# Hyena token convolution: a second fold on 128 rows for the even frequencies, and the filter folds moved ahead of the spectral products

## The reference

```python
def two_sided_fft_conv(u, h_fwd, h_bwd, bias):
    L = u.shape[1]
    kern = jnp.concatenate([h_fwd, jnp.zeros((1, h_fwd.shape[1]), F32), h_bwd[:0:-1]], axis=0)
    uf = u.astype(F32)
    spec = jnp.fft.rfft(uf, n=2 * L, axis=1) * jnp.fft.rfft(kern, n=2 * L, axis=0)[None]
    y = jnp.fft.irfft(spec, n=2 * L, axis=1)[:, :L]
    return (y + uf * bias.astype(F32)).astype(u.dtype)

def hyena_mixer(h, w_in, b_in, short_w, short_b, w1, b1, w2, b2, w3, freq, filt_bias, w_out, b_out):
    L = h.shape[1]
    u = centred_depthwise_conv(h @ w_in + b_in, short_w, short_b)
    v, x1, x2 = jnp.split(u, 3, axis=-1)
    filt = hyena_filters(L, w1, b1, w2, b2, w3, freq)
    z = x1 * two_sided_fft_conv(v, filt[:, 0, 0], filt[:, 0, 1], filt_bias[0])
    z = x2 * two_sided_fft_conv(z, filt[:, 1, 0], filt[:, 1, 1], filt_bias[1])
    return z @ w_out + b_out
```

## Time and profile before

| | us |
|---|---|
| median of 3 runs | 3149.48 (3149.09 to 3150.06) |
| the profiled execution | 3147.32 |
| its span in the trace | 3144.8 |
| PE busy over the span | 2980.0 (95%) |
| DVE busy over the span | 1515.3 (48%) |
| ACT busy over the span | 734.2 (23%) |

### The profile page before, as it was taken

The page is one execution under the profiler, slowest core; times in us unless marked ns, Lnnn a source line. Parts: engine busy times, 40 slices in busy tenths (PEclk is TensorE's granted clock), DMA queues, the critical chain, the costliest instruction groups (busy, mean ns, idle before and its releaser), DMA issues.

```text
span 3144.8 us, 36839 instructions
## 1 busy us (share of the span) xinstructions
PE 2980.0 (95%) x14719; PEld 1696.5 (54%) x14719; DVE 1515.3 (48%) x2905; ACT 734.2 (23%) x1539; POOL 419.9 (13%) x262
## 2 busy tenths in 40 slices
PE   8999899999889899899998999999999987999998
PEld 5888443787744377447756433333345544444443
DVE  5994852898393357775565211211144752111212
ACT  1211541121163221112124111000025642111111
POOL 3554000655200142000001100000000000000000
PEclk9999999999999899999999999999999999999999
DMA  5452002447200322011412899999922004999997
GB/s 227 152 210 81 28 1 108 150 183 279 81 1 14 135 84 110 34 54 37 159 67 86 330 398 399 374 390 378 394 116 78 4 3 174 417 421 421 421 421 291
DMA packets 89899, 606.12 MB, mean 193 GB/s; under 512 B 10808, under 2 KB 11611, under 8 KB 19204
## 3 DMA queue, kind: packets, MB, share of 16 engines
q1 hardware_dynamic: 79776, 575.70, 45.8%
q0 software_dynamic: 4432, 15.73, 1.7%
q10 hardware_dynamic: 5524, 12.35, 1.1%
HBM read 592.73 MB, written 11.01 MB: 192 GB/s over the span
## 4 chain that ended last, share of the span: by engine, by line
PE 63%; DVE 7%; ACT 2%; issue 1%; ACTq 0%; DMA 0%; DVEq 0%; PEldq 0%
PE ps L3054 7%; PE ps L3016 7%; PE ps L1451 4%; PE ps L3067 4%; PE ps L3033 4%; PE ps L3097 4%; PE ps L1098 3%; PE ps L1600 3%; PE ps L3361 2%; PE ps L2904 2%; PE ps L1701 2%; PE ps L3106 2%; PE ps L2820 2%; PE ps L2921 2%; PE ps L1972 2%; PE ps L3525 1%
## 5 line engine op out<-in xcount | busy, mean ns | idle before, releaser
L617 PE MATMUL ps<-mem 128*128 128x256 f32 x1792 | 393.1, 381 | 12.9 <-DVE mem L647 10.8
L617 PEld LDWEIGHTS ps<-mem 128*128 128x128 f32 x1792 | 340.1, 191 | 65.3 <-DVE mem L647 14.4
L562 POOL TENSOR_TENSOR mem<-mem 128x512 f32<-128x512 f32 (+1 forms) x160 | 299.5, 1872 | 535.9 <-DVE mem L858 274.6
L760 DVE SCALAR_TENSOR_TENSOR mem<-mem 128x1024 f32<-128x1024 f32 x160 | 256.5, 1644 | 14.4 <-DMA mem<-in_ada_w 13.9
L3054 PE MATMUL ps<-mem 128*64 128x512 f32 x1024 | 223.3, 594 | 0.0
L3016 PE MATMUL ps<-mem 128*64 128x512 f32 x1024 | 222.5, 592 | 0.7 <-ACT mem L2950 0.7
L647 DVE TENSOR_TENSOR mem<-ps,mem 128x256 f32<-128x256 f32 x308 | 121.5, 419 | 111.7 <-PE ps L617 68.2
L1098 PE MATMUL ps<-mem 128*128 128x512 f32 x384 | 169.6, 597 | 1.8 <-DVEq L156 1.8
L3218 DVE TENSOR_TENSOR mem<-ps,mem 128x512 f32<-128x512 f32 x16 | 11.1, 692 | 313.7 <-PE ps L3016 313.7
L3054 PEld LDWEIGHTS ps<-mem 128*64 128x64 f32 x1024 | 72.1, 137 | 150.5 <-issue 150.5
L3016 PEld LDWEIGHTS ps<-mem 128*64 128x64 f32 x1024 | 74.4, 137 | 145.6 <-issue 144.7
(11 more groups left out here) (455 smaller groups left out, 4393.9 us busy)
## 6 DMA issues: line engine op xcount, KB each, us to landing
mem<-in_moe_w SPq DMA_DIRECT2D x384, 1024.0 KB, 15.3
mem<-in_w_in SPq DMA_DIRECT2D x48, 1024.0 KB, 7.2
mem<-in_ada_w SPq DMA_DIRECT2D x48, 1024.0 KB, 5.0
mem<-in_hy_w_in SPq DMA_DIRECT2D x24, 1024.0 KB, 7.0
mem<-in_w_out SPq DMA_DIRECT2D x12, 1024.0 KB, 6.0
mem<-in_k_win_l SPq DMA_DIRECT2D x8, 1024.0 KB, 6.9
mem<-in_hy_w_out SPq DMA_DIRECT2D x8, 1024.0 KB, 4.9
mem<-in_sw_w_in SPq DMA_DIRECT2D x6, 1024.0 KB, 8.2
```

The costliest lines, as they stand in the source:

```text
L562: gp(out, x, y, op).then_inc(A.mark(sem), 1)
L617: m = mm(seven(l, unit), x[:, k, :], y[:, k, :], start=(k == 0), stop=(k == 3))
L760: stt(PRODUCT if again else w, w, 1.0, C_ROWS[:, z, :], ALU.mult, ALU.mult, accum_out=mod(layer, b // KD, b % KD, z))\
```

## The change

For the even frequencies the 256 folded rows are symmetric about their middle a second time, up to a sign that depends on which half of the even frequencies is meant. So the kernel now orders the even frequencies by their parity (first every other one, then the rest), stores the second tile of 128 rows mirrored (`place`, in the tables and the window; `pe_filter` reads the taps of tile 1 from the mirrored array, and `fold` writes the second 128 places of the data reversed), and forms the sum and the difference of the two tiles. An even output then needs one matmul over 128 rows: `PAIRED` says for kinds 0 and 2 and each g whether it takes the sum or the difference.

- `dve_filter_pair` makes the sum and the difference of the filter in place, four operations, each after the one before, once for each unit. `pair` makes those of the data into `DATA_PAIRS`, four additions, once for each unit.
- PE's spectrum(n) waits for `filter_paired` instead of `filter_folded`, and PE leaves the stage before only when unit 0's pair is made. PE's data(n) waits for `data_paired` too.
- The filter folds of unit 1 move from the middle of products(0) to the place ahead of them, in the loop over b for n = -1.
- The data's first fold is four operations of 4x128 instead of eight of 256.
- The inverse keeps its matmuls; only the order of its tables' rows changes.

```diff
+        place = t
+        if n == "l":
+            even = np.concatenate([even[0::2], even[1::2]])
+            place = np.concatenate([t[:P], t[P:][::-1]])
...
+        fwd = [x[place] for x in fwd]
...
+            if j:
+                h, lo = (y.HR, y.HR, y.H2, y.H2)[m], y.L + 1 - P - lo
...
+        PAIRED = {0: (0, 1), 2: (1, 0)}
+
+        def dve_filter_pair(A, y):
+
+            for m in (HEP, HOM):
+                x, r = y.HE[:, m, 0, :], y.HE[:, m, 1, :]
+                A.e.wait_ge(*A.last)
+                tt(x, x, r, ALU.add).then_inc(A.mark(), 1)
+                A.e.wait_ge(*A.last)
+                stt(r, r, -2.0, x, ALU.mult, ALU.add).then_inc(A.mark("filter_paired" if m == HOM else None), 1)
...
             st.done(A)
-            A.e.wait_ge(S["filter_folded"], TOK.ne)
+            A.e.wait_ge(S["filter_paired"], 1)
...
                 dve_token_pair(A, j, between)
+            dve_filter_pair(A, TOK)
             for j in range(20, 24):
                 dve_token_conv(A, j)
...
             def spectrum(n):
-                A.e.wait_ge(S["filter_folded"], ne * n)
+                if n:
+                    A.e.wait_ge(S["filter_paired"], n)
...
-                    for t in range(ne):
-                        m = mm(ps[:, i % 4, :], y.FWD[:, kind, t, g * P:(g + 1) * P], y.HE[:, FILTER_OF[kind], t, :],
-                               start=(t == 0), stop=(t == ne - 1))
+                    if kind in PAIRED:
+                        m = mm(ps[:, i % 4, :], y.FWD[:, kind, 0, g * P:(g + 1) * P], y.HE[:, FILTER_OF[kind], PAIRED[kind][g], :],
+                               start=True, stop=True)
+                    else:
...
             def data(n):
                 c, o = UNITS[n]
                 A.e.wait_ge(S["turned_out"], 2 * ne * (n + 1))
+                A.e.wait_ge(S["data_paired"], n + 1)
...
+                        if kind in PAIRED:
+                            m = mm(ps[:, 4 + 2 * (i % 2) + part, :], y.FWD[:, kind, 0, g * P:(g + 1) * P],
+                                   DATA_PAIRS[:, 2 * DATA_OF[kind] + PAIRED[kind][g], :], start=True, stop=True)
+                            continue
...
                 for i in range(2 * ne):
-                    if (n, i) == (0, ne):
-                        for b in range(2 * ne):
-                            dve_filter_fold(A, y, b // 2, b % 2)
-                        A.e.wait_ge(*A.last)
...
+                u = y.U3[:, 4 * c:4 * c + 4, :]
+                for part, op in enumerate((ALU.add, ALU.subtract)):
+                    tt(y.FOLD[:, part, :, 0:P], u[:, :, 0:P], u[:, :, L - P:L][:, :, ::-1], op).then_inc(A.mark(), 1)
+                    tt(y.FOLD[:, part, :, P:H], u[:, :, P:H][:, :, ::-1], u[:, :, H:H + P], op)\
+                        .then_inc(A.mark("data_folded" if part else None), 1)
+
+            def pair(n):
+                x = y.natural(UNITS[n][0])
+                A.e.wait_ge(S["turned_out"], 2 * ne * (n + 1))
+                for part in range(2):
+                    for i, op in enumerate((ALU.add, ALU.subtract)):
+                        tt(DATA_PAIRS[:, 2 * part + i, :], x[:, 2 * part, :], x[:, 2 * part + 1, :], op)\
+                            .then_inc(A.mark("data_paired" if part and i else None), 1)
...
                 if n < 0:
                     A.e.wait_ge(S["turned"], 2 * ne)
+                    pair(0)
...
-                    if 0 <= n <= LAST - 2 and b < 2 * ne:
+                    if n + 2 <= LAST and b < 2 * ne:
                         dve_filter_fold(A, y, b // 2, b % 2)
+                        if b == 2 * ne - 1:
+                            dve_filter_pair(A, y)
+                    if 0 <= n < LAST and b == 1:
+                        pair(n + 1)
```

More of the change, by code:

```diff
@@ L101, in shape_constants @@
         win[:L] = np.exp(-tt * deltas) + np.float32(0.05)
-        four = np.stack([win[t], win[t + 1], win[L - 1 - t], win[L - t]], axis=1)
+        four = np.stack([win[t], win[t + 1], win[L - 1 - t], win[L - t]], axis=1)[place]
         c[f"win_{n}"] = np.ascontiguousarray(four.reshape(-1, P, 4, 2, 512).transpose(3, 0, 1, 2, 4).reshape(-1, P, WCH))
@@ L185 @@
               "aux_full", "aux_act", "aux_dve", "sel_scaled", "pair_map", "ctx_map", "product", "inverted", "spread", "selected"]
[L188 removed]
+SHARED_SEMS = {"filter_paired": "scores", "data_paired": "maxima", "h_scaled": "ctx_o_full", "h_shifted": "ctx_o_out", "centre_made": "ctx_hidden", "sums_made": "ctx_full", "v_moved": "ctx_out", "v_stepped": "ctx_turned", "masked": "ctx_silu"}
 def build(nc, a, out):
@@ L1684, in build @@
         C_GAIN = MISC[:, 40:48]
+        DATA_PAIRS = v(TSUM_, 4, 512)
         C_SQ, C_RS, C_H = v(HE_, KD, TC), v(HT_, TC), v(HT_ + 2048, KD, TC)
@@ L1699, in spectrum @@
                         A.e.wait_ge(S["act_out"], 4 * ne * n + i - 3)
-                    for t in range(ne):
-                        m = mm(ps[:, i % 4, :], y.FWD[:, kind, t, g * P:(g + 1) * P], y.HE[:, FILTER_OF[kind], t, :],
-                               start=(t == 0), stop=(t == ne - 1))
+                    if kind in PAIRED:
+                        m = mm(ps[:, i % 4, :], y.FWD[:, kind, 0, g * P:(g + 1) * P], y.HE[:, FILTER_OF[kind], PAIRED[kind][g], :],
+                               start=True, stop=True)
+                    else:
+                        for t in range(ne):
+                            m = mm(ps[:, i % 4, :], y.FWD[:, kind, t, g * P:(g + 1) * P], y.HE[:, FILTER_OF[kind], t, :],
+                                   start=(t == 0), stop=(t == ne - 1))
                     m.then_inc(A.mark("psum_full"), 1)
@@ L1852, in fold @@
                 c = UNITS[n][0]
-                for b in range(4):
-                    u = y.U3[:, 4 * c + b, :]
-                    tt(y.FOLD[:, 0, b, :], u[:, 0:H], u[:, H:L][:, ::-1], ALU.add).then_inc(A.mark(), 1)
-                    tt(y.FOLD[:, 1, b, :], u[:, 0:H], u[:, H:L][:, ::-1], ALU.subtract)\
-                        .then_inc(A.mark("data_folded" if b == 3 else None), 1)
+                u = y.U3[:, 4 * c:4 * c + 4, :]
[10 more added lines that the diff above has]
+                            .then_inc(A.mark("data_paired" if part and i else None), 1)
             def filters(n):
```

1 line of the change is left out of this document (removed).

## The result

| | before | after |
|---|---|---|
| median of 22 runs each, us | 3148.60 | 3152.14 |
| the profiled execution (its span), us | 3147.32 (3144.8) | 3149.90 (3148.1) |
| PE busy, us | 2980.0 | 2961.9 |
| DVE busy, us | 1515.3 | 1535.8 |
| first token pair to first matmul of the context projection, in the trace, us | 353.3 | 358.7 |

The ratio of the runs is 1.0014, with a 95% interval of 1.0008 to 1.0020: 4.4 us slower, 2.5 to 6.3 by the interval (the two medians lie 3.5 us apart). 3155.1 was forecast, from 3150.0 to 3160.0. "The stage" from here on is the stretch of the table's last row, from the first token pair to the first matmul of the context projection. The two traces put the loss where the prediction had it: from the first token pair to the last token product they run alike (128.6 us in each), and what follows up to the context projection is 5.4 us longer.

A forecast was written before the change was run, and what follows sets the result against it. DVE was taken to set the pace from the gates to the fourth data group. Start (-3.95 + L), two rounds (1.14 + L) and unit 3 (0) summed to +5.6 us on 3149.48, so 3155.1 us, range 3150.0 to 3160.0.

The forecast's parts named there:

- DVE sets the pace up to the fourth data group: From the gates to the fourth data group PE waits for DVE, so the 3.46 us cut from data brings nothing.
- The additions: On DVE, pair takes 2.45 us and filter_pair about 3.0; products start 5.2 us later in a round.
- T: The inverse's start, from which a round is counted; products started at T + 21.96 before, forecast T + 27.16.
- Start: Stage's start up to inverse(0): -3.95 + L, +0.3 us, with 3.8 us of PE idle before spectrum(0).
- L: Mean time at the lower clock after a PE restart: 4.2 us, from 2.9 to 5.6; costs L/2.
- Rounds: Rounds 0 to 1 and 1 to 2, between inverses: each 0.57 + L/2, +2.7 us; two rounds +5.4.
- Unit 3: Last unit: pair fits between two gates, 0 us, up to +1.6 if idle lowers the clock.
- The rival with the clock up: Clock stays up over PE's new waits: start -2.8, rounds 2 x 1.74, together +0.7, 3150.1 us; chance 0.10.
- The sum: Whole change: 2L - 2.8, +5.6 us at L = 4.2, giving 3155.1 us; forecast case's chance 0.74.

The follow-up runs named there:

- e1: The changed kernel with the even data kinds taking two matmuls again, pairs still made and waited for: 3157.68 us against 3146.54 before, ratio 1.0040; traced again 3154.89.
- e6: The changed kernel with the filter pair of units 1 to 3 made behind the second product group: 3145.61 us against 3148.55 before, ratio 0.9993.
- after_again: The changed kernel run again, unaltered: 3151.29 us against 3147.91 before, ratio 1.0010.
- e3: The changed kernel without the filter pair, so only data uses the second fold: 3155.15 us against 3146.54 before, ratio 1.0030.
- e5: The changed kernel with unused filler matmuls in PE's waits before spectrum(0) and the third data groups: 3148.42 us against 3148.55 before, ratio 1.0002.
- e7_all: The changed kernel reordered: odd frequencies first, both pairs made later, two fold halves behind the filters: 3136.24 us against 3148.55 before, ratio 0.9964.
- e9_fold_early: As e8_all_start, with unit 3's data fold ahead of products(2) and one token convolution behind filters(1): 3128.88 us against 3147.91 before, ratio 0.9945.
- e4: The kernel before with only unit 1's filter folds moved ahead of products(0): 3143.71 us against 3146.54, ratio 0.9991.
- e2: The changed kernel without the data pairs, so only the spectrum uses the second fold: 3146.35 us against 3146.54 before, ratio 0.9998.
- e8_all_start: As e7_all, with unit 0's filter pair and four token convolutions moved to the Hyena stage's start: 3132.39 us against 3148.55 before, ratio 0.9953.

## Why the prediction held, point by point

- **DVE sets the pace up to the fourth data group.** Right. e1 shows it from PE's side (32 records more, the third group of unit 1 to a hundredth in its place), e6 from DVE's (2.9 us moved, 2.9 us less wait).
- **The additions.** `pair` measured 2.49 us for 2.45. `dve_filter_pair` took four steps of 0.73, 2.9 us for 3.0: the scalar_tensor_tensor in place lasts 0.69 us here, not the 0.75 of the earlier trace rows. Products(1) started at T + 26.79 for T + 27.16; the 0.37 us are that and closer packing.
- **Start.** Predicted -3.95 + L with a mean L of 4.2. With the two L measured, 3.4 and 5.9 us, it gives -3.95 + 4.65 = +0.7; measured +0.65. Spectrum(0) waited 3.74 us for the 3.8. The idle ahead of unit 0's third group was 9.88 us, not over 10: the data group before it ran slow as well (6.10 us for 8 records) and so ended later, which cost nothing. In after_again, where it took 5.37, the idle was 10.61.
- **Rounds.** Predicted 0.57 + L/2 = 2.7 each. With L of 3.5 and 5.8 it gives 2.3 and 3.5; measured 1.94 and 3.02, less the same 0.4 us of the chain in both.
- **Unit 3.** Predicted 0; measured -0.23. The wait of 2.42 us left the clock at 1.00 in both traces of after. In e3 and e6 it fell there, and unit 3 came out 0.5 and 0.3 us longer than after's, well under the 1.6 allowed, since the next wait for DVE takes most of it up. That it stayed up in after was luck as far as the rows went, a small one by these prices.
- **The rival with the clock up** was costed at start -2.8, rounds 2 x 1.74, together +0.7. e5 made this case: -2.3, +1.4, +1.4, stage +0.3. So the split between work (near 0) and clock (about +5) was right too.
- **The sum.** +5.6 forecast; +5.4 and +4.5 in the stage of the two traces of after, +4.4 and +3.1 by the ratios. The forecast was made against a median of three runs at 3149.48; with 22 runs it is 3148.60, which is another 0.9 us between 3155.1 and 3152.14. That 5.6 met 5.4 so closely is partly luck: the four low times of after had a mean of 4.65 us and not 4.2, the packing of the chain took 0.8 us back, and the same program traced again gave 4.5. That a shift of the stage's end passes on whole was assumed. Between before and after 2.1 us of it are not in the span (3.3 for 5.4), within the scatter of the rest; the larger shifts of e7_all and e9_fold_early arrived whole (-12.0 and -18.7 us in the stage, -12.3 and -19.0 in the runs).
- **What it did not see.** It netted the start in one formula, and so hid that moving the folds alone gains 5.3 us there (e4) and that pairing the data then loses 3.9 us of it (e2 against after). It also took the additions' place as given. e6 shows that the place decides the sign (+5.4 to -2.8 us), and e7 to e9 go further with it.
- **What stays open.** No run puts the kernel before, without the second fold, into e9_fold_early's order, so how much of the 18.7 us needs the second fold isn't shown. An estimate from its rows: before's PE is busy for 335.6 us of the stage, 2.6 of it lost to the lower clock (16.51 us for the spectrum at 1291.31 against 13.91), so it would have to lose all but 1.6 of its 17.7 us of idle to reach 334.6. The move of the folds (e4) took 5.2 us off.

The Trainium skill, page "Perfetto Trace Analysis", section "Identifying the Most-Contended Engine", says of the busy share of matmuls that it is not a good measure of how close a kernel is to the roofline. That is a rule on the roofline; what the prediction took from it, that a tensor engine may be busy nearly all the time and not set the pace, is shown here by e1: 32 records put back into a stage in which PE is busy 317 of 359 us left its length within 0.6 us as it was, once the clock's two timings are matched. The page "TensorE: Matmul & The Clock Gate" of the Trainium skill, section "HAM oscillation — how this bites in real kernels", describes matmul bursts that fall back to the slow clock at each wait and pay each time. Here e5 measures 5.1 us for four waits; the fifth, of 2.42 us in unit 3, did not lower the clock in after.

## What to carry to other kernels

Before taking work off an engine that is 95% busy, look at where it waits and who is late there: here a transform halved by extra additions cost time while the additions stood in the chain that the busy engine waits for, and the kernel gained once they stood where the helping engine idles or the busy one has work of its own. Order the groups so that those which need no extra preparation come first, and put the preparation of the others behind the first products; here this turned +5 us into -19 us in the stage with the same work on each engine. Read a small net change by its parts, since it can be a gain of 5 and a loss of 10.

## What the runs showed of the hardware that I had not expected

- **The wait's length alone doesn't say whether the clock falls.** Behind a wait of 2.42 us it stayed at 1.00 in after; behind the same wait, at the same place, it fell in e3_data_only and e6_pair_late. Behind 1.7 us in the filters of round 0 it stayed up in e8_all_start and fell in e9_fold_early. Even one kernel does both: in e8_all_start it fell behind the same 1.71 us one unit earlier (0.79 over the 8 us from 1299.34), and in e2_spec_only, behind 3.22 us ahead of the third data group, it stayed at 1.00 in round 0 and fell to 0.81 in round 1. Windows of 8 us from the restarts (4.64 in after, above), of e3_data_only, e6_pair_late, e8_all_start and e9_fold_early:

```profile
1447.81:1455.81 8.00, 8.00 (x15) 3.55 (x16) 7.86 (x14) 0.00 (x0) 0.00 (x0) 0.79 0.01 3
```

```profile
1438.65:1446.65 8.00, 8.00 (x15) 3.60 (x16) 7.86 (x14) 0.00 (x0) 0.00 (x0) 0.80 0.00 0
```

```profile
1348.51:1356.51 8.00, 7.72 (x36) 5.02 (x36) 7.18 (x12) 2.33 (x4) 0.00 (x0) 1.00 0.01 2
```

```profile
1348.10:1356.10 8.00, 8.00 (x32) 5.38 (x33) 6.30 (x11) 2.17 (x4) 0.00 (x0) 0.79 0.01 2
```

- **The time at the lower level varied from 3.4 to 5.9 us in after** behind waits of 3.7 to 9.9 us, and not with the wait: 6.83 us were followed by 3.5 us in one round and by 5.8 in the next. Both rounds did so in both traces of after. What picks it is open.
- **Identical programs ahead of a change differ by some microseconds from kernel to kernel** (the first token pair started between 1114.3 and 1120.3 us in the 13 traces), so an effect of a few microseconds is better read from the parts of the stage than from the whole.
